# Hybrid attention block on one core: half of a scaling and most of the probability multiplies go to GpSimd, and one compression is moved

## The reference

```python
h = rms_norm(x, g_pre_mix) * (1.0 + sc1) + sh1
proj = h @ w_in
q, kc, vc, ksl, vsl, kwn, vwn, nsa_g, u, br_g = jnp.split(proj, IN_SPLITS, axis=-1)
kc_c = compress(rope(kv(kc)), cmp_pe_k, cmp_w1_k, cmp_w2_k)   # blocks of 32 keys, gelu(blk @ w1) @ w2
vc_c = compress(kv(vc), cmp_pe_v, cmp_w1_v, cmp_w2_v)
# three branches per head: compressed blocks, selected blocks, a window of 512 keys
p = masked_softmax(q . k * scale)            # e / max(sum(e), 1e-30), for each branch
o = g_cmp * p_cmp @ v_cmp + g_sel * p_sel @ v_sel + g_win * p_win @ v_win
```

## Time and profile before

| | |
|---|---|
| median of three runs | 1478.3 us (1478.2 to 1479.91) |
| the profiled execution, its own time | 1479.48 us |
| its span, first to last instruction | 1477.7 us |
| mean granted PE clock | 0.991 |
| busy share PE, DVE, ACT, POOL | 96%, 72%, 44%, 22% |
| chain that ended last, share by engine | PE 80%, DVE 10%, ACT 3% |

### The profile page before, as it was taken

The page is one execution under the profiler, slowest core; times in us unless marked ns, Lnnn a source line. Parts: engine busy times, 40 slices in busy tenths (PEclk is TensorE's granted clock), DMA queues, the critical chain, the costliest instruction groups (busy, mean ns, idle before and its releaser), DMA issues.

```text
span 1477.7 us, 19532 instructions
## 1 busy us (share of the span) xinstructions
PE 1414.5 (96%) x7206; PEld 1182.6 (80%) x7206; DVE 1070.7 (72%) x1479; ACT 646.5 (44%) x1124; POOL 328.6 (22%) x429
## 2 busy tenths in 40 slices
PE   3898999999999999989999999999999999999997
PEld 3786778888888888768887877888888888888885
DVE  5759844677877878885432788877777797777778
ACT  4534524555665666663122664222222434343342
POOL 2314432333322322111210410000000030404034
PEclk9999999999999999999999999999999999999999
DMA  9377856322221211016453424544443773535226
GB/s 354 89 244 256 266 121 169 86 75 60 64 62 47 57 56 34 19 63 194 142 182 103 143 75 156 197 157 156 147 145 136 270 286 113 199 109 204 87 84 228
DMA packets 131750, 208.31 MB, mean 141 GB/s; under 512 B 19525, under 2 KB 84549, under 8 KB 128071
## 3 DMA queue, kind: packets, MB, share of 16 engines
q1 hardware_dynamic: 128074, 196.61, 40.6%
q0 software_dynamic: 3584, 10.49, 2.1%
HBM read 146.24 MB, written 54.53 MB: 136 GB/s over the span
## 4 chain that ended last, share of the span: by engine, by line
PE 80%; DVE 10%; ACT 3%; issue 3%; SPq 2%; DMA 2%; POOL 0%; DVEq 0%; POOLq 0%; ACTq 0%
PE ps L2071 17%; PE ps L2072 17%; PE ps L2073 17%; PE ps L2077 5%; PE ps L2078 5%; PE ps L2079 5%; PE ps L2271 4%; PE ps L2287 2%; PE ps L2288 2%; PE ps L2238 2%; PE ps L2239 2%; DVE acc L1559 1%; DMA ada<-in_w_ada 1%; SPq L539 1%; DVE ada_acc L1434 1%
## 5 line engine op out<-in xcount | busy, mean ns | idle before, releaser
L2071 PE MATMUL ps<-act_hi,a_hi 128*128 128x512 f32 x448 | 190.8, 426 | 0.5 <-DVE a_lo L1413 0.5
L2073 PE MATMUL ps<-act_hi,a_lo 128*128 128x512 f32 x448 | 175.6, 392 | 0.0
L2072 PE MATMUL ps<-act_lo,a_hi 128*128 128x512 f32 x448 | 175.2, 391 | 0.0
L2071 PE MATMUL ps<-wr_hi,left_hi 128*128 128x512 f32 x320 | 124.5, 389 | 0.0
L2072 PE MATMUL ps<-wr_lo,left_hi 128*128 128x512 f32 x320 | 124.5, 389 | 0.0
L2073 PE MATMUL ps<-wr_hi,left_lo 128*128 128x512 f32 x320 | 124.5, 389 | 0.0
L1615 DVE TENSOR_TENSOR pt_lo<-ps,pt_hi 128x512 fp32r<-128x512 f32 (+1 forms) x160 | 103.1, 644 | 19.8 <-ACT pt_hi L1152 18.3
L1334 ACT ACTIVATE left_hi<-left_st 128x2048 fp32r<-128x2048 f32 x28 | 53.6, 1915 | 144.1 <-PE ps L2073 81.8
L1254 ACT ACTIVATE w_hi<-w1s 128x1024 fp32r<-128x1024 f32 x54 | 57.0, 1057 | 112.3 <-PE ps L2073 74.8
L1152 ACT ACTIVATE pt_hi<-ps 128x512 fp32r<-128x512 f32 (+1 forms) x160 | 89.0, 563 | 32.6 <-PE ps L2271 30.9
L1739 DVE TENSOR_TENSOR w_lo<-w1s,w_hi 128x1024 fp32r<-128x1024 f32 x54 | 65.9, 1222 | 51.1 <-ACT w_hi L1254 51.0
(11 more groups left out here) (282 smaller groups left out, 3882.7 us busy)
## 6 DMA issues: line engine op xcount, KB each, us to landing
left_st<-h_dram SPq DMA_DIRECT2D x28, 1024.0 KB, 5.1
ada<-in_w_ada SPq DMA_DIRECT2D x48, 512.0 KB, 5.9
h_dram<-hid SPq DMA_DIRECT2D x48, 512.0 KB, 3.1
w1s<-in_w_fc SPq DMA_DIRECT2D x32, 512.0 KB, 4.4
w2s<-in_w_fc SPq DMA_DIRECT2D x16, 1024.0 KB, 7.4
raw<-in_w_in SPq DMA_DIRECT2D x28, 512.0 KB, 4.5
g_dram<-g_out POOLq DMA_DIRECT2D x32, 256.0 KB, 2.4
mg<-g_dram SPq DMA_DIRECT2D x16, 512.0 KB, 3.8
```

The costliest lines, as they stand in the source:

```text
L2071: pe.matmul(dst, wh, mh, start=start, stop=False)
L2072: pe.matmul(dst, wh, ml, start=False, stop=False)
L2073: return pe.matmul(dst, wl, mh, start=False, stop=stop)
```

## The change

Three edits. The scaling of x tiles 4 to 7 goes from DVE to POOL, behind all four wv_lo instructions, each right after its tile's two small instructions. compress(0) on PE goes from behind block 4 to between the two halves of block 5. From unit 8 on the multiplies of the probabilities go from DVE to POOL: DVE keeps the reciprocal, POOL multiplies step s - 1 after the guard of step s, and the compressed step of a unit in the next iteration, after its first guard. DVE's reciprocal of step n newly waits for the multiply of step n - 4, as there are four columns of sums and reciprocals.

```diff
+POOL_FROM = 8
...
+        def scale_x(t):
+            pool.wait_ge(x_rstd, 2 * t + 2)
+            pool.tensor_scalar(xt[:, t, :], xt[:, t, :], msq[:, t:t + 1], None, ALU.mult).then_inc(x_norm, 1)
+
         for i in range(4):
             pool.wait_ge(wv_hi_s, i + 1)
             pool.tensor_tensor(wv_lo[:, 2 * i:2 * i + 2, :], wv_raw[:, 2 * i:2 * i + 2, :],
                                full(wv_hi[:, 2 * i:2 * i + 2, :]), ALU.subtract).then_inc(wv_lo_s, 1)
-            if i:
-                x_rstd_of(3 + i)
-        x_rstd_of(7)
+        for t in range(4, TT):
+            x_rstd_of(t)
+            scale_x(t)
         pool.wait_ge(xt_mm, 2 * KT)
...
+        def normalise(u, s):
+            c, n = u // 4, STEPS * u + s
+            pool.wait_ge(rec_done, n + 1)
+            pool.wait_ge(norm_done, n)
+            for x, hh in enumerate((0, 1) if s == 4 else (s % 2,)):
...
+                ins = pool.tensor_scalar(buf[:, u % 2, hh, 0:w], buf[:, u % 2, hh, 0:w], srec[:, n % 4, x:x + 1],
+                                         gates[:, c, at:at + 1], ALU.mult, ALU.mult)
+            ins.then_inc(norm_done, 1)
...
             if it < UNITS:
                 guards(it, 0)
+            if it > POOL_FROM:
+                normalise(it - 1, STEPS - 1)
...
                 for s in range(1, STEPS):
                     guards(it, s)
+                    if it >= POOL_FROM:
+                        normalise(it, s - 1)
...
-        def normalise_x(t):
-            dve.wait_ge(x_rstd, 2 * t + 2)
-            dve.tensor_scalar(xt[:, t, :], xt[:, t, :], msq[:, t:t + 1], None, ALU.mult).then_inc(x_norm, 1)
...
             split_h(h_tmp, n, h_made, h_hi, h_lo)
-            if 2 <= n < 6:
-                normalise_x(n + 2)
...
             dve.wait_ge(guard_done, n + 1)
+            if n >= 4:
+                dve.wait_ge(norm_done, n - 3)
             dve.reciprocal(srec[:, n % 4, 0:k], ssum[:, n % 4, 0:k]).then_inc(rec_done, 1)
+            if u >= POOL_FROM:
+                return
...
             for ch in range(2):
                 g = 2 * a + ch
+                if a == 5 and ch == 1:
+                    compress(0)
...
-            if a == 4:
-                compress(0)
```

More of the change, by code:

```diff
@@ L877, in guards @@
             pool.tensor_scalar(ssum[:, n % 4, 0:k], ssum[:, n % 4, 0:k], 1e-30, None, ALU.max).then_inc(guard_done, 1)
+        def normalise(u, s):
[3 more added lines that the diff above has]
+            for x, hh in enumerate((0, 1) if s == 4 else (s % 2,)):
+                branch = s // 2
+                buf = (p_sel, p_win, p_cmp)[branch]
+                w = cmp_width(c) if s == 4 else sum(q[1] for q in score_parts(c, branch))
+                at = 3 * (2 * (u % 4) + hh) + (1, 2, 0)[branch]
+                ins = pool.tensor_scalar(buf[:, u % 2, hh, 0:w], buf[:, u % 2, hh, 0:w], srec[:, n % 4, x:x + 1],
+                                         gates[:, c, at:at + 1], ALU.mult, ALU.mult)
+            ins.then_inc(norm_done, 1)
         def split_gate_block(a):
```

## The result

Four runs of the changed kernel have a median of 1491.33 us (1489.77 to 1493.76); the kernel before has 1478.25. The ratio is 1.0086, 95% interval 1.0073 to 1.0099: 13 us slower, between 11 and 15. The forecast was 1482.0 with a range up to 1488.0; the direction was right and the size was not. The profiled execution took 1490.38 us, with a span of 1488.6: 10.9 more than the span before.

A forecast was written before the change was run, and what follows sets the result against it. PE was taken as the bound from 190 us, DVE mattering only in the front and last iterations; +5.6 + 0.7 - 2.6 = +3.7 on the median 1478.3 gave 1482.0 us, range 1476.5 to 1488.0.

The forecast's parts named there:

- Term A: Front, scaling x on POOL: last scaling 3.9 us later plus 1.7 for PE's clock, +5.6, between +2.0 and +12.7.
- I take 1.23, as a multiply by a per-partition column reads one tensor: POOL's scaling of one 1024-column x tile: 1.23 us, from its one-input copy of 512 columns, median 0.617.
- 2.59, the two-input row: High price of one POOL scaling of x, from the two-input instruction of 512 columns, median 1.294.
- The clock term: PE after standing some 6 us before the second half's x transposes: lower clock costs 1.7 us, ends 0 and twice that.
- Nothing behind hides it: After the x transposes: memset, bias, weight pieces, additions and projections of h wait for them and move together.
- Term B: First compression moved into block 5: PE's stand moves before the second, which becomes the slow one; +0.7, between 0 and +1.1.
- ACT's earlier copies: ACT's second copy of block 5 comes 0.41 us earlier, and gelu and DVE's blocks with it, lowering +1.1 to +0.7.
- Term C: Multiplies of units 8 to 31 on POOL: gain only in the last iterations and the end, -2.6, between -4.8 and +2.
- pt_hi late next: Iterations 29 to 31: ACT's pt_hi ends at 623.05 against 623.16 for p_sel, so removing 0.81 there buys 0.1.
- 0.4 to spare: Units 8 to 11: POOL's 384-column window multiply, 0.46 us, ends at 320.7, before PE takes the tile at 321.08.
- A wait of PE for POOL's multiplies between 300 and 600 us: Attention iterations: if PE waits there for POOL's multiplies, the prediction counts as wrong.
- The third: Front: POOL becomes the bound, multiply with a column operand at the two-input price; +9.1, 1487.4 us, chance 0.15.

The follow-up runs named there:

- experiment 4: Changed kernel with a second multiply, by a column of ones, in POOL's scaling of x: 1485.27 us, ratio 1.0049 to the kernel before.
- experiment 5: Changed kernel with another form of POOL's multiply for each x tile, run once for its trace: one operation by a constant 2.78 us, two operations 1.12.
- experiment 13: Kernel before with only the scaling moved to POOL, plus 97 unused PE transposes before the second half's x transposes: 1489.88 us, ratio 1.0069.
- experiment 14: Changed kernel plus 97 unused PE transposes in its stand before the second half's x transposes: 1490.81 us, ratio 1.0080 to the kernel before.
- experiment 11: Changed kernel with two multiplies per scaling, plus 43 unused PE transposes before the second half's x transposes: 1484.78 us, ratio 1.0039.
- experiment 3: Kernel before with only the probabilities' multiplies moved to POOL from unit 8 on: 1478.51 us, ratio 0.9995.
- experiment 6: Changed kernel with DVE scaling x again, compression and multiplies as changed: 1480.19 us, ratio 1.0008 to the kernel before.
- experiment 7: Kernel before with only the probabilities' multiplies moved to POOL, from unit 12 on instead of 8: 1475.81 us, ratio 0.9982.

## Why the prediction was wrong

**Term A, the step that failed: "I take 1.23, as a multiply by a per-partition column reads one tensor".** Four scalings took 12.50 us, not 4.92: +7.6. The rest of the working erred the other way, by less: wv_lo ended at 42.28 instead of 43.8, rstd pairs and gaps took 5.12 instead of 5.68, and so the last scaling ended 5.5 later than worked out. The bound failed too: 2.59, the two-input row, was taken as the dear end, but the nearest rows by columns and inputs were rows of other forms, and the form was what mattered: in the same place 2.85 with one operation and 1.19 with two (experiments 4 and 5). In experiment 4, where POOL's price is the predicted one, the transposes start at 54.71; the prediction said 54.4. By the Trainium skill (GPSIMD Engine Reference, section 8, Key points), the vector engine is about twice as fast at elementwise work; against DVE's 0.67 us that holds for the form with two operations (1.19) and not for the one that the change uses (2.85, about four times).

The clock term of +1.7 was about right, but the comparison hides it: the two profiled executions took 16.84 and 16.63 us from transposes to memset, -0.2, because the one before had a stretch at a lower clock of its own there. Against the 15.27 of traces without one the long stand cost 1.4 (experiments 13 and 14). "Nothing behind hides it" was right. Experiments 11 and 14 keep PE busy in the stand, one with the quick form of the scaling and one with the slow one: they are 5.4 us apart at the transposes (54.78, 60.20), 5.4 at the memset (71.62, 77.06) and 5.6 in the times of the profiled executions (1485.23, 1490.81).

**Term B, undersized.** The stand went where it was expected, in front of the second compression, and the dear compression with it. It was 8.3 instead of 6, since the first compression, now quick, puts PE another 1.7 ahead. The price came out at 1.9 in the profiled execution (2.1 alone, 0.7 to 3.4) instead of 0.7. The compression lost 1.62 (5.26 against 3.64), and 0.65 of it was covered, as worked out. Another 1.0 comes from DVE: from the end of the second key blocks to the end of the additions it needed 14.50 us (178.96 to 193.46) where it had needed 15.49 (167.39 to 182.88), so that PE is later against them. That is not shown to be the change's work: the same stretch took 14.54 in experiment 3, where the compression stays, and 15.50 in experiment 6, where it is moved. The 0.4 that the prediction deducted for ACT's earlier copies can't be told from this spread.

**Term C, right in the tail and wrong in one date.** Iterations 29 to 31 last 13.42 us (627.62 to 667.87 in three); 13.4 was worked out, with pt_hi late next, and the row at 644.35 shows DVE waiting for it. The end gave 0.9 (9.35 instead of 10.23 us between the last two outputs) instead of 0.5. What failed is "0.4 to spare". The rows taken were of an iteration before unit 8, where the first window tile comes in a slot of its own. From unit 8 on it shares a slot with the last tile of p_sel, and the trace before shows that: the guard ends at 351.01, PE takes the tile at 351.29, 0.28 later, not 0.98. POOL's multiply of 384 columns took 0.66, not 0.46, and PE waited 0.37 three times and 0.25 once. From the last transposes of p_sel to the first of p_win it is 0.75 us (352.41 to 353.16) where it was 0.22: the overlap of the two is lost as well, 0.5 an iteration, and the four iterations grew by 2.1. A wait of PE for POOL's multiplies between 300 and 600 us was one of the prediction's own signs of being wrong. So the sum of C is -0.7, not -2.6, inside its range.

**Sum.** Predicted +5.6 + 0.7 - 2.6 = +3.7. In the trace: +9.2, +1.9, +2.1 - 2.9, and +1.4 on the way to the end of the additions, together +11.7, of which the span shows 10.9. Of the 7.2 us between +3.7 and 10.9, A has 3.6, B 1.2, C 1.9 and the additions 1.4, less 0.8 that was not followed up. The 1.4 are not shown to be a part of the change: 1.9 is lost before DVE's first key blocks, 0.5 from there to the end of the second ones, and 1.0 is won back in the additions (Term B). Before the first key blocks, from DVE's last step on the gates to these, it took 55.3 us in the profiled execution before (78.13 to 133.40) and 57.2 in the changed one (87.33 to 144.52), but 57.1 and 57.7 in experiments 3 and 7 too, whose programs are those of before up to there. DVE's waits in that stretch for weight pieces of the modulation are 7.6 us before, 9.6 in the changed kernel and 10.0 in experiment 7: the execution profiled before had them early.

**Rivals.** The third came nearest (1487.4), with the right place and the wrong mechanism: it blamed the column operand. That it had the date of the last scaling (59.8; it was 59.90) is luck: 2.59 a scaling was 2.1 us too little for the four, and wv_lo and the rstd pairs were put 2.1 too long. At the measured 2.85 to 3.56 its sum gives over 1489, outside the range.

## What to carry to other kernels

A price for an instruction that the trace doesn't show has to come from a row of the same form, operation count included; where there is none, the range has to allow for several times the nearest row, and a second, idle operation is worth a try. Work may leave an engine only towards one that is done with it by the date of the first reader: read that date in each kind of iteration that the change touches, not in one. Filling a stand in front of work that another engine releases gains nothing, and the engine's lower clock behind the new stand is a cost. Read a stage's length from more than one trace: here the one trace of the kernel before had a lower clock of its own in the stage that the clock term concerns, and only the traces of other kernels, with the same program there, showed it.

## What the runs showed of the hardware

- POOL's multiply of 128x1024 float32 by a column or a constant takes 2.78 to 2.85 us with one operation and 1.12 to 1.19 with two, where nothing else was at work.
- POOL and DVE slow each other. DVE's rounding of a slice of h takes 0.43 us with POOL idle and 1.60 beside POOL's subtraction, which ended at 40.03, 0.29 before it. The single multiply took 3.56 beside DVE's splits and 2.85 alone; inside those 3.56 (43.82 to 47.38) the rounding kept its 0.42:

```profile
38.72 1.60 DVE L1467 CAST act_hi<-h_tmp 128x512 fp32r<-128x512 f32 x1
...
44.28 0.42 DVE L1467 CAST act_hi<-h_tmp 128x512 fp32r<-128x512 f32 x1
...
61.91 0.43 DVE L1467 CAST act_hi<-h_tmp 128x512 fp32r<-128x512 f32 x1 [12.46 <-ACT h_tmp L1032]
```

By the Trainium skill (SBUF — State Buffer, Who interferes with whom), the two share a pair of ports, and when DVE is in a two-port mode the one that comes second waits for the other's whole instruction. The row beside the subtraction agrees with such a wait; the row inside the multiply does not. In which mode DVE was, no run here shows.
- The same short wait of PE is followed by a lower clock in some executions and not in others. In experiment 11 PE stood 1.96 us up to 63.79, and the granted clock was 0.63 from 64 to 66 and 0.51 from 66 to 68. The kernel before has this wait up to 59.56, with 0.72 and 0.50 from 60 to 64 behind it; the changed kernel has it up to 70.30, and no fall behind it (1.00 from 64 to 76). No run here shows what decides.
